# Rotary partners by transfers within SBUF, issued by ACT, and a new order of work around them

## The chip, the cores and the metric

One NeuronCore of a Trainium2 chip runs the whole computation. The metric is the device time of one execution in microseconds; less is better. The engines are PE (TensorE, matrix products), DVE (VectorE), ACT (ScalarE), POOL (GpSimd) and SP (SyncE, which here only issues transfers). The on-chip memory SBUF and the accumulators in PSUM are the two places where data stands between instructions.

## The reference

x is 512 tokens by 1024 columns. It goes through one block of a first kind and then two layers of a second kind, all in float32.

```
# first block
u = rmsnorm(x, ln1_g);  q,k,v,pool_in,z,xbc,dt,gate = split(u @ w_in)
y_a = dilated_attention(q,k,v)   # 3 groups (dilation 1, 4, 16) of 6 heads; the groups' outputs o_g = (p @ v) / l
                                 # are mixed by softmax over the groups of lse_g = max + log(l)
y_b = pool_mixer(pool_in);  y_c = ssd_mixer(z, xbc, dt)
x = x + (gates[0]*y_a + gates[1]*y_b + gates[2]*y_c) @ w_o
x = x + conv_ffn(rmsnorm(x, ln2_g));  x = rmsnorm(x, final_g)
# second block, two layers
u = rms_norm(h, attn_norm[l]);  dq,dk,dv,rq,rk,rv,rg,gq,gk,gv,gates = split(u @ w_in_2[l])
dq, dk = partial_rope(rms_norm(dq)), partial_rope(rms_norm(dk))   # first 16 of each 64
rq, rk = apply_rope(rq), apply_rope(rk)                           # all 128
gq, gk = axial_rope(rms_norm(gq)), axial_rope(rms_norm(gk))       # 32 + 32 of each 64
a, r, c = differential_attention, bidirectional_retention, grouped_query_attention
h = h + sum(gates * (a, r, c) @ w_branch) @ w_out
h = h + square(relu(rms_norm(h, mlp_norm[l]) @ w_mlp_in)) @ w_mlp_out

def apply_rope(x, cos_sin):      # halves x1, x2 of a block
    return concatenate([x1 * cos - x2 * sin, x2 * cos + x1 * sin])
```

## The kernel before

**Products.** Activations lie transposed in SBUF, channels on partitions and the 512 tokens along the free dimension. Each float32 product with weights is made of three products of rounded parts (high x high, high x low, low x high). A chunk of weights is 128 x 1024: SP loads it into one of four slots (`load`), ACT rounds it to its high part (`high`, line 715), DVE or, from the second block on and for every other chunk, POOL subtracts to get the low part (`low`, line 720; `low_pool`, line 751), and PE makes 24 matrix products with it in 3 "thirds" of 8. `high` and `low` called for one chunk treat the chunk three further on. Products with weights accumulate in a ring of four PSUM banks (`G`), all other work of PE in a second ring of four (`M`): a group opens when the group four before it in the ring has been read. Each engine executes its own list in order.

**Filling.** The attention parts are chains over PE, DVE and ACT with gaps for PE. So the projections that come later are cut into thirds, and an order written out by hand (`attn_steps`, `ssd_steps`, `gqa_steps`, `diff_steps`, `ret_steps`) says after which step PE makes how many thirds (`fill(n)`). ACT and DVE do their share of a filling chunk when their own list comes to a step by whose mark PE has finished it (`Follow.to`).

**Block 1.** Units u = 0 to 8 of the dilated attention (three groups of three pairs of heads): scores on PE, bias and maxima on DVE (`front`), exponentials with row sums on ACT, normalising on DVE (`normalise`, lines 1729 and 1733: the reciprocal of the sums, then four scalings for each of two heads), transposes on PE, their copies on ACT, the product with v on PE. `logs(g)` transposes max and log of a group; after the last group DVE and ACT form the softmax over the groups (lines 1769 to 1786) and PE spreads it over the heads (`alpha`, line 1564). The SSD scan follows, later the FFN (`ffn_act`, `ffn_dve`), whose first gating chain runs on ACT and DVE while PE makes the second pair of up products.

**A layer of the second block.** Rotated tiles come in three kinds: g (6 tiles, grouped attention), d (8, differential attention) and r (8, retention). The g tiles stand at the head of the layer, with no filling work: rope_pe, rope_act and rope_dve go tile by tile, then v of the grouped attention is copied (line 2851) and its scores begin. The d and r tiles are filling work: the d tiles fall in the grouped attention, the r tiles in the differential attention. For a tile x, ACT copies and scales it from PSUM to `raw` and squares it for the norm, PE forms the sums of squares (`ss`, line 2701, not for r) and multiplies `raw` with a matrix of zeros, ones and minus ones (`rot`, line 2704), which puts into each half of a block the other half. DVE multiplies `raw` with the cosines, the rotated copy in PSUM with the sines (line 2785), adds them and applies the norm's root (`finish`). ACT may overwrite one of the two `raw` buffers for tile x once `finish(x - 2)` is done, which comes on DVE behind the low part of the next chunk.

**The attention parts of a layer.** Grouped and differential attention have 16 steps each: scores on PE, maxima on DVE, exponentials on ACT (line 2914 for the grouped one), weights on DVE, transposes on PE (line 2868), copies on ACT, and per head or pair a product with v. Retention ends with the mean and the variance of each head, two products with a matrix of ones (`mean`, `var`, line 3168).

Of the kernel before, what the change touches and what calls it, by code (L numbers as in the profile page):

```python
# [25 lines left out]
P = 128  # L26
S = 512
# [36 lines left out]
def const_pack():  # L64
# [14 lines left out]
    def rot(n, half, block):  # L79

        r = np.zeros((P, P))
        for b in range(0, P, block):
            for j in range(half):
                r[b + j, b + j + half] = -1.0
                r[b + j + half, b + j] = 1.0
        return r.T
    put("rot_d", rot(16, 8, 64))
    put("rot_r", rot(128, 64, 128))
    put("rot_g", rot(32, 16, 32))
# [31 lines left out]
def rope_pack():  # L121
# [6 lines left out]
    out[0, :, 0] = 1.0  # L128
    a = table(t, 16, 500000.0)
    for b in (0, 64):  # L130
        out[0, b:b + 16, 0] = np.cos(np.concatenate([a, a]))
        out[0, b:b + 16, 1] = np.sin(np.concatenate([a, a]))
    a = table(t, 128, 10000.0)
    out[1, :, 0], out[1, :, 1] = np.cos(np.concatenate([a, a])), np.sin(np.concatenate([a, a]))
    for b in (0, 64):
        for o, q in ((0, t // 64), (32, t % 64)):
            a = table(q, 32, 10000.0)
            out[2, b + o:b + o + 32, 0] = np.cos(np.concatenate([a, a]))
            out[2, b + o:b + o + 32, 1] = np.sin(np.concatenate([a, a]))
# [94 lines left out]
def attn_steps(score, turned, value, logs, vturn, dtturn, alpha, fill):  # L234

    for u in range(10):
# [21 lines left out]
    logs(2)  # L258
    fill(6)
# [5 lines left out]
def ssd_steps(bturn, xturn, decay, seg, pair, yturn, fill):  # L265

    bturn(0)
    fill(1)
    bturn(1)
    fill(2)  # L270
# [3 lines left out]
    for n in range(18):  # L274
# [9 lines left out]
        fill(1 if n < 11 else 0)  # L284
# [18 lines left out]
def order_block1():  # L303
# [29 lines left out]

    def pair(c, x):
# [6 lines left out]
    attn_steps(score, turned, lambda v: M.add("o", v), lambda g: M.add("lT", g), lambda: [M.add("vt", t) for t in range(NT)],  # L341
# [63 lines left out]

def diff_steps(score, turned, value, mean, fill):

    for u in range(20):
# [7 lines left out]
        fill(2 if u < 17 else 0)  # L416
# [4 lines left out]
def ret_steps(score, value, mean, var, fill):  # L421
# [14 lines left out]
    fill(2)  # L436
    var(3)
    fill(2)
# [29 lines left out]
def order_layer(c1, g1, m1, first):  # L468
# [7 lines left out]
    def post(kind, t):  # L476
        if kind != "r":
            M.add("ss", kind, t)
        M.add("rot", kind, t)
# [109 lines left out]
def build(nc, a, out, consts, attn_consts, ropes, dists, line_dram):  # L589
# [435 lines left out]
    def merge_act(st, n, kt, l=None, final=False):  # L1025
        e, m0 = st.e, merge_count(n, l)

# [372 lines left out]
    lT = kb("lT", [HG, 3, S], 94)  # L1400
    lx = kb("lx", [HG, 2, S], 100)
# [87 lines left out]
    def attn_pe(pe, fill):  # L1489
# [17 lines left out]
        def turned(v, m):  # L1507
            pe.wait_ge(sem("prob_ready"), 2 * v + m + 1)
# [24 lines left out]
        def logs(g):  # L1533
# [67 lines left out]
    def attn_act(st, follow):  # L1601
# [49 lines left out]
        dt_log_act(st)  # L1651
        follow("al", 0)
        for g in range(3):
            e.wait_ge(sem("lmax_ready"), g + 1)
            st.f(e.activation(lT[:, g, :], lT[:, g, :], ACT.Exp), sem("lexp_ready"), g + 1)
        for m in range(3):
# [17 lines left out]
    def attn_dve(st, follow):  # L1674
# [48 lines left out]
        def normalise(v):  # L1723
            g, t = v // 3, v % 3
            w = 256 if g == 0 else P
            for m in range(2):
                h = 2 * t + m
                e.wait_ge(sem("exp_ready"), 2 * v + m + 1)
                st.s(e.reciprocal(stat[:, g, 2, :, h], stat[:, g, 1, :, h]))
# [4 lines left out]
                st.w()  # L1734
                e.sem_inc(sem("prob_ready"), 1)

        def logs(g):
# [3 lines left out]
            gr.done(st, e.tensor_copy(perm(lT[:, g, :], DIL[g]), res(o[0:HG, :], DIL[g])))  # L1741

        for u in range(10):
            if u > 0:
                normalise(u - 1)
                if u % 3 == 0:
                    g = u // 3 - 1
                    e.wait_ge(sem("ln_ready"), g + 1)
# [1893 lines left out]
```

## Time and profile before

| | |
|---|---|
| median of 3 runs | 3173.43 us (3172.94 to 3173.64) |
| the profiled execution | 3172.14 us, of which the span of the trace is 3170.2 us |
| PE busy | 96% of the span, 13152 matrix instructions |
| DVE, ACT, POOL busy | 49%, 40%, 12% |
| mean granted clock of TensorE | 0.981 of full speed |

Busy is the time in which an engine executes at least one instruction. Products overlap on PE, so their mean durations add up to more than they cost; the distance from one start to the next is the cost. A wait is idle time of an engine just before an instruction, put down to what ended it.

### The profile page before, as it was taken

What the parts mean: (1) busy time and instruction counts of PE and PEld (TensorE: products, weight loads), DVE (VectorE), ACT (ScalarE), POOL (GpSimd) and SP (SyncE); (2) the same over time, 40 slices, a digit from 0 to 9 for tenths busy, and PEclk for the clock granted to TensorE, in tenths of its full rate; (3) what the DMA queues carried; (4) which work ended last, traced back from release to release, by engine and by line L of the source; (5) the groups of instructions that cost most, each with busy time, mean ns of one, the idle gap of its engine ahead of it and who ended that gap; (6) DMA issues with size and microseconds to landing.
All of it is one profiled execution on the core that took longest, in us unless ns stands there. A gap on an engine that the chain in (4) does not pass through costs nothing. (4 is left out here: it accounts for less than half of the span.)

```text
span 3170.2 us, 35921 instructions
## 1 busy us (share of the span) xinstructions
PE 3037.3 (96%) x13152; PEld 2332.6 (74%) x13152; DVE 1566.0 (49%) x2166; ACT 1257.5 (40%) x1861; POOL 392.6 (12%) x233
## 2 busy tenths in 40 slices
PE   7997899999999998899999999999899999999998
PEld 6876678888778775566676888887556676788887
DVE  3547667545754666545533551434544633453242
ACT  3445325333433454544444432234554453342221
POOL 4000000000000001011111222221101111222221
PEclk9998899999999999999999999999999999999999
DMA  7222113333323331122222333333112222233332
GB/s 187 80 68 60 42 45 94 99 94 102 91 86 103 88 95 47 40 67 67 71 70 68 99 93 99 94 98 94 39 41 80 65 76 67 80 100 100 93 99 86
DMA packets 460160, 259.02 MB, mean 82 GB/s; under 512 B 20202, under 2 KB 452172, under 8 KB 460016
## 3 DMA queue, kind: packets, MB, share of 16 engines
q1 hardware_dynamic: 454064, 246.03, 26.9%
q0 software_dynamic: 5952, 11.13, 1.4%
q8 instruction: 84, 1.38, 0.2%
q14 instruction: 60, 0.49, 0.1%
HBM read 254.98 MB, written 5.64 MB: 82 GB/s over the span
## 5 line engine op out<-in xcount | busy, mean ns | idle before, releaser
L715 ACT ACTIVATE wH<-wR 128x1024 fp32r<-128x1024 f32 (+1 forms) x476 | 491.3, 1032 | 475.3 <-DMA wR<-in_w_mlp_out_dram 196.9
L720 DVE TENSOR_TENSOR wL<-wR,wH 128x1024 fp32r<-128x1024 f32 (+1 forms) x332 | 396.0, 1193 | 509.0 <-ACT wH L715 492.6
L751 POOL TENSOR_TENSOR wL<-wR,wH 128x1024 fp32r<-128x1024 f32 (+1 forms) x144 | 346.0, 2403 | 2002.9 <-ACT wH L715 2002.9
L782 PE MATMUL ps<-uH,wH 128*128 128x512 f32 x1176 | 483.9, 411 | 5.0 <-DVE wL L720 3.6
L782 PE MATMUL ps<-uL,wH 128*128 128x512 f32 x1176 | 482.7, 410 | 0.0
L782 PE MATMUL ps<-uH,wL 128*128 128x512 f32 x1176 | 479.4, 408 | 0.0
L770 PE MATMUL ps<-uH,wH 128*128 128x512 f32 x976 | 386.0, 395 | 8.8 <-DVE wL L720 7.5
L770 PE MATMUL ps<-uL,wH 128*128 128x512 f32 x976 | 381.2, 391 | 0.0
L770 PE MATMUL ps<-uH,wL 128*128 128x512 f32 x976 | 380.9, 390 | 0.0
L782 PEld LDWEIGHTS ps<-uH,wH 128*128 128x128 f32 x1176 | 226.7, 193 | 78.7 <-issue 24.2
L782 PEld LDWEIGHTS ps<-uH,wL 128*128 128x128 f32 x1176 | 226.9, 193 | 71.3 <-issue 26.1
L782 PEld LDWEIGHTS ps<-uL,wH 128*128 128x128 f32 x1176 | 226.7, 193 | 70.6 <-issue 26.3
L770 PE MATMUL ps<-mH,wH 128*128 128x512 f32 x688 | 268.0, 390 | 2.1 <-DVE wL L720 2.1
L770 PE MATMUL ps<-mL,wH 128*128 128x512 f32 x688 | 267.8, 389 | 0.0
L770 PE MATMUL ps<-mH,wL 128*128 128x512 f32 x688 | 267.8, 389 | 0.0
L770 PEld LDWEIGHTS ps<-uH,wH 128*128 128x128 f32 x976 | 183.9, 188 | 56.6 <-DVE wL L720 16.9
L770 PEld LDWEIGHTS ps<-uL,wH 128*128 128x128 f32 x976 | 183.9, 188 | 38.6 <-issue 1.4
L770 PEld LDWEIGHTS ps<-uH,wL 128*128 128x128 f32 x976 | 183.8, 188 | 38.6
L770 PEld LDWEIGHTS ps<-mH,wH 128*128 128x128 f32 x688 | 129.2, 188 | 29.7 <-DVE wL L720 2.9
L770 PEld LDWEIGHTS ps<-mL,wH 128*128 128x128 f32 x688 | 129.2, 188 | 26.8
L770 PEld LDWEIGHTS ps<-mH,wL 128*128 128x128 f32 x688 | 129.2, 188 | 26.7
L3412 ACT ACTIVATE mH<-msc 128x512 f32 x64 | 40.5, 632 | 235.7 <-DVEq L3448 235.7
(469 smaller groups left out, 4266.4 us busy)
## 6 DMA issues: line engine op xcount, KB each, us to landing
wR<-in_w_in_dram SPq DMA_DIRECT2D x185, 512.0 KB, 3.7
wR<-in_w_mlp_in_dram SPq DMA_DIRECT2D x64, 512.0 KB, 4.0
wR<-in_w_mlp_out_dram SPq DMA_DIRECT2D x64, 512.0 KB, 4.0
wR<-in_ffn_w_up_dram SPq DMA_DIRECT2D x44, 512.0 KB, 3.8
wR<-in_w_branch_dram SPq DMA_DIRECT2D x24, 512.0 KB, 3.4
wR<-in_w_out_dram SPq DMA_DIRECT2D x16, 512.0 KB, 4.1
wR<-in_ffn_w_down_dram SPq DMA_DIRECT2D x16, 384.0 KB, 3.4
wR<-in_ffn_w_down_dram SPq DMA_DIRECT2D x16, 320.0 KB, 3.0
```

The costliest lines, as they stand in the source:

```text
L715: st.f(st.e.activation(wH[:, slot, 0:n], wR[:, slot, 0:n], ACT.Copy), hi_ready, c + 1)
L720: st.f(st.e.tensor_tensor(wL[:, slot, 0:n], wR[:, slot, 0:n], wH[:, slot, 0:n].bitcast(F32), ALU.subtract), lo_ready, c + 1 if done is Non ...
L751: e.tensor_tensor(wL[:, slot, 0:n], wR[:, slot, 0:n], wH[:, slot, 0:n].bitcast(F32), ALU.subtract).then_inc(sem("lo_pool"), 1)
L770: ins = pe.matmul(outp, w[:, k, c0:c0 + m], x[:, k0 + k, :], start=k0 == 0 and s == 0, stop=k0 + kt == kn and s == len(steps) - 1)
L782: ins = pe.matmul(o[:, :], w[:, k, :], x[:, k, :], start=s == 0, stop=s == 3 * KD - 1)
L3412: st.f(e.activation(mHf[:, ds((4 * i + j) * S, S)], msc[:, j % 2, :], ACT.Copy), sem("hidH_ready"), x + 1)
```

## The change

The three rotation matrices leave the constants. The signs go into the sine table, and the exchange of halves is done by transfers from `raw` to a new buffer `partner`, issued by ACT right behind the copy and square of a tile: two per block, so 8 for a g tile, 4 for a d tile, 2 for an r tile. DVE's `finish` waits for them and reads `partner`. For the r tiles the buffer is `sg`, which the gates use otherwise, so two waits are added there.

In the dilated attention the weights are no longer normalised before their product with v. The reciprocal of the row sums is taken once for each group, transposed like the logs (`rT`), and multiplied into the factors of the groups. The logs of the last group move ahead of the last unit.

The rest moves work: thirds in `ssd_steps`, `diff_steps`, `ret_steps`; in `gqa_steps` each step begins with the transposes of two steps before, and its scores come after the first third; in the FFN two weight conversions go from behind the first gating chain to right behind the norm.

```diff
@@ attn_steps
+        if u == 9:
+            logs(2)
+            fill(2)
         turned(u - 1, 0)
-        fill(2 if u < 9 else 3)
+        fill(2)
         turned(u - 1, 1)
...
-    logs(2)
-    fill(6)
+    fill(5)
@@ ssd_steps
     bturn(0)
-    fill(1)
+    fill(2)
     bturn(1)
-    fill(2)
+    fill(3)
...
-        fill(1 if n < 11 else 0)
+        fill(1 if n < 9 else 0)
@@ gqa_steps
     for u in range(19):
-        if u < 16:
-            score(u)
-        fill(1)
         if u >= 6 and u % 4 == 2:
             value(u // 4 - 1)
         if 2 <= u < 18:
             turned(u - 2)
+        fill(1)
+        if u < 16:
+            score(u)
         fill(1)
@@ diff_steps
-        fill(2 if u < 17 else 0)
+        fill((1 if u % 4 == 1 else 2) if u < 17 else 0)
@@ ret_steps
     mean(3)
-    fill(2)
+    fill(5)
     var(3)
-    fill(2)
+    fill(3)
@@ merge_act
+        if l is not None and n == 0:
+            e.wait_ge(sem("rope_done"), 22 + 22 * l)
@@ attn_pe
         def turned(v, m):
-            pe.wait_ge(sem("prob_ready"), 2 * v + m + 1)
+            pe.wait_ge(sem("exp_ready"), 2 * v + m + 1)
...
+            gr = M("rT", g)
+            o = gr.open(pe)
+            for n in range(NT):
+                ins = pe.transpose(o[0:HG, n * P:(n + 1) * P], stat[:, g, 2, n, :], C("ident"))
+            gr.close(ins)
@@ attn_act: the exponentials of lT now stand before dt_log_act and follow("al", 0)
@@ attn_dve
-        def normalise(v):
...
-                for n in range(4):
-                    x = scores_at(v)[:, m, n * w + (P if g == 0 and n == 0 else 0):(n + 1) * w]
-                    st.s(e.tensor_scalar(x, x, stat[:, g, 2, n, h:h + 1], None, ALU.mult))
...
+            if u > 0 and u % 3 == 0:
+                g = u // 3 - 1
+                e.wait_ge(sem("ln_ready"), g + 1)
+                st.s(e.reciprocal(stat[:, g, 2, :, :], stat[:, g, 1, :, :]))
...
+            if u == 9:
+                logs(2)
...
+        st.w()
+        for g in range(3):
+            st.s(e.tensor_tensor(lT[:, g, :], lT[:, g, :], rT[g][:, :], ALU.mult))
@@ ssd_dve: spread(0) moves ahead of the four xt steps
@@ ffn_act
                     normed_u_act(st, u_base("ffn"), 0, G("up", 0, 0, 1))
+                    high(st, ("up", 0, 0, 1))
+                    high(st, ("up", 0, 1, 0))
@@ ffn_dve: low(...) for the same two
@@ rope_post_pe
-        g = M("rot", kind, t, l=l)
         o = g.open(pe)
-        g.close(pe.matmul(o[:, :], C(ROT[kind]), raw[kind][:, x % 2, :], start=True, stop=True))
+        g.close(pe.matmul(o[:, :], C("blk64"), sq[:, x % 2, :], start=True, stop=True))
...
+    HALVES = {"d": (8, (0, 64)), "r": (64, (0,)), "g": (16, (0, 32, 64, 96))}
+    def swap_act(st, kind, x, l):
+
+        half, firsts = HALVES[kind]
+        src, dst = raw[kind][:, x % 2, :], partner[kind][:, x % 2, :]
+        for f in firsts:
+            for a, b in ((f, f + half), (f + half, f)):
+                st.e.dma_start(dst[a:a + half, :], src[b:b + half, :]).then_inc(sem(f"partner_in{x % 2}"), 16)
@@ rope_act, g tiles 0 and 1
                 e.sem_inc(sem("raw_tile"), 1)
+                swap_act(st, kind, x, l)
                 if x > 0:
                     root(x - 1)
@@ rope_act, the other tiles
             e.sem_inc(sem("raw_tile"), 1)
+            if kind == "r" and x == 0:
+                e.wait_ge(sem("sg_free"), 2 + merge_count(2, l) + 8)
+            swap_act(st, kind, x, l)
             if norm and x > 0:
                 root(x - 1)
             high(st, (kind, t), l)
@@ rope_dve
         def finish(x):
...
-            g.done(st, e.tensor_tensor(raw[kind][:, x % 2, :], o[:, :], table[:, S:2 * S], ALU.mult))
-            st.w()
-            st.s(e.tensor_tensor(y, y, raw[kind][:, x % 2, :], ALU.add))
+            e.wait_ge(sem(f"partner_in{x % 2}"), partner_in(kind, x, l))
+            st.w()
+            st.s(e.tensor_tensor(z, z, table[:, S:2 * S], ALU.mult))
+            st.w()
+            st.s(e.tensor_tensor(y, y, z, ALU.add))
@@ gqa_act, gqa_dve: each step in the order of the new gqa_steps (copies of the transposes, then exponentials)
```

## Rows read from the trace of the kernel before

**Rows 1.** The page, busy time of each engine over the whole span.

```profile
PE 3037.3 (96%) x13152; PEld 2332.6 (74%) x13152; DVE 1566.0 (49%) x2166; ACT 1257.5 (40%) x1861; POOL 392.6 (12%) x233
```

**Rows 2.** Busy time in one window: us, then each engine's busy us (instructions), clock.

```profile
1900.00:2000.00 100.00, 100.00 (x443) 82.86 (x442) 22.04 (x26) 20.36 (x20) 21.54 (x9) 1.00 0.33 95
```

**Rows 3.** Waits of PE, whole span: us in total, times, longest.

```profile
PE ps L1564 <- DVEq L1788: 14.9, 1, 14.9
PE ps L3168 <- ACT nrmt L3190: 12.0, 2, 6.2
PE ps L1528 <- ACTq L1648: 11.2, 3, 7.4
PE ps L2868 <- DVE raw L2785: 10.6, 6, 2.9
...
PE ps L2701 <- ACT gpr L2914: 7.6, 6, 2.2
...
PE ps L2868 <- ACT gpr L2914: 6.3, 3, 2.9
PE ps L2027 <- DVEq L2114: 5.5, 3, 2.3
...
PE ps L2704 <- ACTq L2765: 3.3, 2, 1.8
```

**Rows 4.** Line 2704: ns minimum/median/maximum of one, first and last start.

```profile
L2704 PE MATMUL ps<-raw,cn x56: 592/592/1061, 1196.2 to 2349.6; 128*128 128x512 f32 x56
...
L2704 PE MATMUL ps<-raw_r,cn x32: 590/592/697, 1489.1 to 2545.3; 128*128 128x512 f32 x32
```

**Rows 5.** Timeline of PE at 1208 us: start, us, engine, line, count.

```profile
1207.99 1.02 PE L2701 MATMUL ps<-sq,cn 128*128 128x512 f32 x2
1208.85 1.02 PE L2704 MATMUL ps<-raw,cn 128*128 128x512 f32 x2
```

**Rows 6.** Timeline of SP's first issues.

```profile
0.75 0.39 SPq L1178 DMA_DIRECT2D cn<-table_consts_dram  x1
1.19 0.36 SPq L1179 DMA_DIRECT2D grow<-in_ln_g_dram  x1
```

**Rows 7.** Timeline of POOL, two small issues in one row.

```profile
13.72 0.96 POOL L1189 DMA_DIRECT2D prow<-in_gqa_k_norm_dram  x2
```

**Rows 8.** DMA issues: size of one, median us to landing.

```profile
cn<-table_consts_dram SPq DMA_DIRECT2D x1, 64.0 KB, 1.9
```

**Rows 9.** Timeline of ACT in the head of the first layer.

```profile
1193.80 0.63 ACT L2746 ACTIVATE sq<-raw 128x512 f32<-128x512 f32 x1 [1.84 <-DVEq L2800]
...
1198.33 1.06 ACT L715 ACTIVATE wH<-wR 128x1024 fp32r<-128x1024 f32 x1 [0.18 <-ACT rs L878]
1203.13 0.69 ACT L2760 ACTIVATE raw<-ps,lp 128x512 f32<-128x512 f32 x1 [3.73 <-DVEq L2793]
...
1223.72 0.69 ACT L872 ACTIVATE rs<-ps,cn 128x512 f32<-128x512 f32 x1 [2.15 <-PE ps L2701]
...
1227.43 0.60 ACT L2851 ACTIVATE gvf<-ps 128x512 f32<-128x512 f32 x1
```

**Rows 10.** Busy time in two stages of the first layer, columns as in rows 2.

```profile
1229.00:1390.00 161.00, 144.16 (x578) 87.73 (x579) 87.70 (x135) 81.23 (x151) 15.75 (x7) 0.94 0.14 40
1390.00:1580.00 190.00, 186.85 (x773) 130.56 (x770) 99.27 (x148) 84.97 (x144) 30.07 (x14) 1.00 0.25 73
```

**Rows 11.** Groups of DVE by line: busy us, mean ns.

```profile
L1733 DVE TENSOR_SCALAR sc<-sc,stat 128x128 f32<-128x128 f32 (+1 forms) x64 | 15.2, 302 | 0.9
...
L1783 DVE RECIPROCAL lx<-lx 6x512 f32<-6x512 f32 x1 | 3.3, 3342 | 0.0
...
L1786 DVE TENSOR_TENSOR lT<-lT,lx 6x512 f32<-6x512 f32 x3 | 1.9, 674 | 0.0
```

**Rows 12.** Timeline of ACT at the first gating chain of the FFN.

```profile
815.39 1.06 ACT L715 ACTIVATE wH<-wR 128x1024 fp32r<-128x1024 f32 x1
```

**Rows 13.** Timeline of PE at the same place.

```profile
818.24 0.79 PE L770 MATMUL ps<-uH,wH 128*128 128x512 f32 x1 [7.04 <-DVE wL L720]
```

More of the change, by code:

```diff
@@ L332, in turned, with logs @@
             M.add("t", v, m, b)
+    def logs(g):
+        M.add("lT", g), M.add("rT", g)
     def pair(c, x):
@@ L340, in order_block1 @@
     none = lambda n: None
-    attn_steps(score, turned, lambda v: M.add("o", v), lambda g: M.add("lT", g), lambda: [M.add("vt", t) for t in range(NT)],
+    attn_steps(score, turned, lambda v: M.add("o", v), logs, lambda: [M.add("vt", t) for t in range(NT)],
                lambda: M.add("dtT"), lambda m: [M.add("al", m, g) for g in range(3)], none)
@@ L1400, in build @@
     lT = kb("lT", [HG, 3, S], 94)
+    rT = [kb(f"rT{g}", [HG, S], (72, 76, 88)[g]) for g in range(3)]
     lx = kb("lx", [HG, 2, S], 100)
@@ L1655, in attn_act @@
             st.f(e.activation(lT[:, g, :], lT[:, g, :], ACT.Exp), sem("lexp_ready"), g + 1)
+        dt_log_act(st)
+        follow("al", 0)
         for m in range(3):
@@ L1764, in attn_dve @@
                 dt_front_dve(st)
-        dt_mid_dve(st)
-        logs(2)
-        st.w()
-        st.s(e.tensor_tensor(lx[:, 0, :], lT[:, 0, :], lT[:, 1, :], ALU.max))
-        st.w()
-        st.s(e.tensor_tensor(lx[:, 0, :], lx[:, 0, :], lT[:, 2, :], ALU.max))
-        st.w()
-        for g in range(3):
-            st.s(e.tensor_tensor(lT[:, g, :], lT[:, g, :], lx[:, 0, :], ALU.subtract))
-            st.w()
-            e.sem_inc(sem("lmax_ready"), 1)
         follow("al", 0)
@@ L1786, in attn_dve @@
             st.s(e.tensor_tensor(lT[:, g, :], lT[:, g, :], lx[:, 1, :], ALU.mult))
+        st.w()
+        for g in range(3):
+            st.s(e.tensor_tensor(lT[:, g, :], lT[:, g, :], rT[g][:, :], ALU.mult))
         st.w()
@@ L2539, in ffn_dve @@
                     normed_u_dve(st, u_base("ffn"), 0, ffn_gain, 1)
+                    low(st, ("up", 0, 0, 1))
+                    low(st, ("up", 0, 1, 0))
                 for t, cv in ((0, cva), (1, cvv)):
@@ L2781, in finish @@
             y = qk[kind][:, order[x], :]
-            g = M("rot", kind, order[x], l=l)
-            o = g.take(e)
+            z = partner[kind][:, x % 2, :]
+            e.wait_ge(sem(f"partner_in{x % 2}"), partner_in(kind, x, l))
             st.w()
-            g.done(st, e.tensor_tensor(raw[kind][:, x % 2, :], o[:, :], table[:, S:2 * S], ALU.mult))
+            st.s(e.tensor_tensor(z, z, table[:, S:2 * S], ALU.mult))
             st.w()
-            st.s(e.tensor_tensor(y, y, raw[kind][:, x % 2, :], ALU.add))
+            st.s(e.tensor_tensor(y, y, z, ALU.add))
             if norm:
@@ L2905, in gqa_act @@
         for u in range(19):
-            if u < 16:
-                follow("gs", u)
-                e.wait_ge(sem("gmax_ready"), 16 * l + u + 1)
-                if u >= 3:
-                    e.wait_ge(misc_ready, M("gt", u - 3, 1, l=l).nth)
-                st.w()
-                for m in range(2):
-                    g = M("gs", u, m, l=l)
-                    g.done(st, e.activation(gpr[:, u % 3, m, :], g.ps[:, :], ACT.Exp, bias=gst[:, u % 3, m:m + 1],
-                                            accum_out=gst[:, u % 3, 2 + m:3 + m]))
-                st.w()
-                e.sem_inc(sem("gexp_ready"), 1)
             if u >= 6 and u % 4 == 2:
@@ L2937, in gqa_act @@
                 e.sem_inc(sem("gt_turned"), 1)
+            if u < 16:
+                follow("gs", u)
+                e.wait_ge(sem("gmax_ready"), 16 * l + u + 1)
+                if u >= 3:
+                    e.wait_ge(misc_ready, M("gt", u - 3, 1, l=l).nth)
+                st.w()
+                for m in range(2):
+                    g = M("gs", u, m, l=l)
+                    g.done(st, e.activation(gpr[:, u % 3, m, :], g.ps[:, :], ACT.Exp, bias=gst[:, u % 3, m:m + 1],
+                                            accum_out=gst[:, u % 3, 2 + m:3 + m]))
+                st.w()
+                e.sem_inc(sem("gexp_ready"), 1)
     def gqa_dve(st, l, follow):
@@ L2941, in gqa_dve @@
         for u in range(20):
+            if u >= 6 and u % 4 == 2:
+                p = u // 4 - 1
+                follow("gpv", p)
+                g = M("gpv", p, l=l)
+                e.wait_ge(sem("bH_ready"), 27 + 20 * l + p + 1)
+                st.w()
+                g.done(st, e.tensor_tensor(bgL[:, p, :], g.ps[:, :], bgH[:, p, :].bitcast(F32), ALU.subtract))
+                st.w()
+                e.sem_inc(sem("b_ready"), 1)
+            if 2 <= u < 18:
+                follow("gt", u - 2)
             if 1 <= u < 17:
@@ L2951, in gqa_dve @@
                 e.sem_inc(sem("gw_ready"), 1)
-            if u >= 7 and u % 4 == 3:
-                p = u // 4 - 1
-                follow("gpv", p)
-                g = M("gpv", p, l=l)
-                e.wait_ge(sem("bH_ready"), 27 + 20 * l + p + 1)
-                st.w()
-                g.done(st, e.tensor_tensor(bgL[:, p, :], g.ps[:, :], bgH[:, p, :].bitcast(F32), ALU.subtract))
-                st.w()
-                e.sem_inc(sem("b_ready"), 1)
             if u < 16:
```

68 lines of the change are left out of this document (27 added, 41 removed).

## The prediction

> **What bounds the kernel now.** I read the page first [rows 1]: PE is busy 96% of the span, DVE about half and ACT 40%. So nearly every microsecond of PE work taken away where PE is never idle comes off the time, and every microsecond that DVE or ACT takes costs nothing unless PE waits for it. A window in the middle of the MLP gives the price of a product: 443 products in 100 us of unbroken work [rows 2], 0.226 us each; a "third" of a filling piece is 8 of them, 1.81 us. Next the list of waits of PE [rows 3], because most of this change moves work in order to shorten one of them. Last the timeline, for what ACT and DVE do in the short stretch at the head of each layer where no filling work exists. There PE, ACT and DVE run as one chain from tile to tile.
>
> **What goes: the rotation products.** The 88 records of line 2704 [rows 4] are 44 products of two records each (22 tiles in each of two layers, an f32 product having two). Their busy time, 46 us, overlaps; a pair starts 0.86 us after the pair ahead of it [rows 5]. That is 44 x 0.86 = 37.8 us of PE. Twelve of the 44 are g tiles, done in the head of a layer where another chain sets the pace, and I count them at nothing; if PE sets the pace there they are 5.2 us a layer. The 16 others of a layer are d tiles (8, during the grouped attention) and r tiles (8, during the differential attention, where PE is nearly never idle).
>
> **What comes: 192 transfers issued by ACT.** A g tile needs 8 (four blocks, two halves), a d tile 4, an r tile 2: 48 + 32 + 16 = 96 a layer. The trace has no transfer issued by ACT. The nearest rows are small ones from SP, 0.39 and 0.36 us each [rows 6], and from POOL, 0.48 us [rows 7]. ACT executes in order, so an issue there is time in which no activation starts. I take 0.41 us, between SP and POOL; the bounds are 0.36 and 0.50. Nothing in the trace excludes a far lower price on ACT, which is a rival below. Data that small lands in about 2 us (64 KB took 1.9 [rows 8]); DVE needs a tile's partner only after ACT has done the next tile's copy, so the landing is hidden, even at twice that.
> The page "DMA: Bandwidth & Descriptors" of the Trainium skill (section "Anatomy of one DMA") puts the dispatch by the sequencer at about 50 ns. SP's rows here are seven times that; by the page's figure the sum below would come to some 3105 us.
>
> **The head of a layer (g tiles).** Before [rows 9]: ACT squares and scales tile 0 from 1193.80 us, the same for tile 1, then takes the root of tile 0 and converts the weights of the fifth product at 1198.33; DVE's low part follows (1.2 us for a full chunk), so PE starts at about 1200.8. After: 8 issues stand behind tile 0's copy and 8 behind tile 1's, both ahead of that conversion: 16 x 0.41 = 6.6 us, so PE starts at about 1207.4. From there each tile runs: ACT's copy and square (1.3), 8 issues (3.3), the root of the tile before (1.4), the weights' high part (0.6 to 1.1), DVE's low part (0.7 to 1.2) and the rotation's end (2.2), after which ACT may overwrite the buffer with the tile after next. The wait of 3.73 us at 1203.13 for DVE shows this chain. Four more tiles add 4 x 3.3 = 13.1 us, 19.7 with the first 6.6. About 4.3 of it disappears in time that ACT spends waiting for PE's sums (2.15 at 1223.72, with two smaller ones) and in the last step, where the copy of v no longer follows rotations. So the copy of v, at 1227.43 before, comes at about 1243: +15 us in each layer. At 0.36 it is +13, at 0.50 +20. In such gaps PE's clock falls to its half level for some products, which the chain mostly hides.
>
> **Grouped attention (d tiles).** Per layer PE loses 8 x 0.86 = 6.9 us of work. PE's rotation groups also leave the ring of four PSUM slots: the 10.6 us in which transposes waited for a rotation's slot to be read by DVE (line 2785) [rows 3] go with them, 5.3 a layer. Against it ACT gets 32 x 0.41 = 13.1 us more. In this stretch ACT is busy 81 of 161 us [rows 10], but its exponentials are what PE waits for (7.6 and 6.3 us in [rows 3]): a tile's copy, issues, root and conversion are one piece of 5.4 us between two exponentials. The new step order brings each transpose forward: three fills after its scores in place of five. Chain: maxima 1.5, exponentials 1.9, weights 1.5 us, against 3 x 1.81 of fill; it holds only when no such piece falls in between. I take 0 for the stage: -12.2 (work and slots) against about +12 (issues that show). Bounds: -12 if all the issues hide, +12 if the shorter lag shows as well.
>
> **Differential attention and retention.** 8 rotations, 6.9 us, where PE was 98% busy [rows 10], and its wait for ACT's raw r tile (3.3 in two layers, line 2704 [rows 3]): -8.5 a layer. The two issues of an r tile, 0.8 us, lie under the filling work. Four thirds move from the differential steps to the end of retention: mean(3) is followed by 5, not 2, and var(3), for which PE waited 12.0 us in two layers [rows 3], gets 3 x 1.81 = 5.4 us more cover: -5.4 and about -0.6 for the half clock after such a gap, -6 a layer. The differential steps keep 7 thirds of 8 in one step of four, and PE waits nearly nothing there, so I count that at 0; without that cover it would be 1.8 a step.
>
> **Block 1.** Attention: normalising goes from DVE: its scalings alone take 15.2 us over nine units [rows 11], with reciprocals and gaps 2.2 us a unit; it stood ahead of the maxima that ACT's exponentials wait for. Two of the three waits of line 1528 (11.2 in all [rows 3]) and one at line 1514 follow such a unit: 3 x 2 = -6. The transposed reciprocals add 12 transposes, at most 3 us, I take +1. The wait for alpha, 14.9 us, looks as if it went altogether, since the logs move up; but DVE's last convolution piece before it ends with a product that PE finishes one third (1.8 us) before alpha. After that DVE needs 4.4 (convolution, silu, low part) and then two additions 1.4, the reciprocal 3.3, three products 1.9 [rows 11] and three more new ones 1.9: with ACT's 0.8 and the gaps between them 14 us, less 1.8: 12.3 left. -2.6. Together -8 (between -14, if alpha's wait goes, and 0). SSD: one third more ahead of each of the first waits, one less in steps 9 and 10, where DVE was already late (5.5 us in three waits of line 2027 [rows 3]): -1 (-4 to +4). FFN: the weights of the fifth up product were converted only at 815.39, behind the whole first gating chain, and PE stood 7.0 us [rows 12, 13]; moved behind the norm they are ready at 811. -7, and -2 for products at half clock after it (the first record lasts 0.79 us in place of 0.39): -9. Block 1: -18.
>
> **Sum.** A layer: +15 + 0 - 8.5 - 6 = +0.5. Both layers and block 1: +1 - 18 = -17. From the profiled execution, 3172.1 us (span 3170.2), this is 3155; the median of the runs shown is 1.3 above it, so **3156 us**, 0.5% faster.
>
> **Rivals.** (1) Issues on ACT cost next to nothing. Then the head of a layer stays as it is (0), the grouped attention gives -10, the rest -14.5: 2 x -24.5 - 18 = -67, 3106 us. For it: no row of the trace rules it out. Against it: SP and POOL both show 0.36 us or more for the smallest. 13%. By the 50 ns of the Trainium skill this would be the likeliest case. (2) Slower: ACT becomes the bound of the grouped attention. The place is the piece of copy, issues, root and conversion in front of an exponential; price: 1.6 us of issues and 1.4 of the lost lag for each of 8 tiles, 12 us a layer over my sum; with issues at 0.50 in the head, 5 more. 3156 + 2 x 17 = 3190 us. It decides from about 12 us a layer above my forecast. For it: PE's waits for line 2914; against it: ACT is half idle there. 20%. (3) The gains of block 1 are paid back in the layers, the stage sums a few us worse than mine: 3173 us, 16%. It needs the head at +20 and grouped attention at +4. (4) The forecast, 3130 to 3166 around 3156: 51%.
>
> **How the numbers follow.** No change that this kernel's measurement can tell is within 0.2%, 3167 to 3180 us. Faster: (4) and (1), 64%. Same: (3), 16%. Slower: (2), 20%. The range leaves out the cheap end of (1) and the dear end of (2): 3106 to 3188.
>
> **What would show it.** ACT's queue should show transfers 0.4 us apart; in the head, the copy of v should come some 15 us later behind the first g tile than before (34 us then). From the first score of grouped attention to the first of differential attention it should take about what it took, 165 us (1228.7 to 1393.5 us). The retention's wait for line 3168 should fall from 6 to about 0.5 us, the FFN's 7.0 to 0, alpha's from 14.9 to about 12. Transfers landing in 5 us or more, or issues far from 0.41 us, would make the forecast wrong.

## The result, and the profile after

The changed kernel takes 3239.7 us (median of 4 runs, 3235.8 to 3241.9) against 3173.5 us on the same chip: a ratio of 1.0207, 95% interval 1.0189 to 1.0225. It is 66 us slower. The forecast was 3156 us, range 3106 to 3188: wrong in sign and outside its range.

The page of the profiled execution (3241.9 us, granted clock 0.966), against [rows 1]:

```profile
span 3240.1 us, 35849 instructions
...
PE 3039.5 (94%) x13076; PEld 2339.8 (72%) x13076; DVE 1538.9 (47%) x2085; ACT 1260.6 (39%) x1863; POOL 391.3 (12%) x233
```

PE is busy as long as before, with 76 matrix instructions fewer: what it lost in work it got back in products at half clock (326 of its products with weights last over 0.6 us, where 220 did before), and 68 us of idle time came on top (the span's 69.9 less 2.2). ACT's busy time is unchanged too, because issuing a transfer isn't counted as busy in these profiles. So the busy times hide the cause; the timeline of ACT at the head of the first layer shows it (columns as in [rows 9], which are the same instructions before):

```profile
1187.47 0.63 ACT L2759 ACTIVATE sq<-raw 128x512 f32<-128x512 f32 x1 [1.84 <-DVEq L2817]
1188.13 0.72 ACT L2761 ACTIVATE raw<-raw,lp 128x512 f32<-128x512 f32 x1
1188.96 5.10 ACTq L2717 DMA_DIRECT2D partner<-raw  x8
1194.11 0.63 ACT L2759 ACTIVATE sq<-raw 128x512 f32<-128x512 f32 x1 [5.25 <-issue]
...
1195.60 5.00 ACTq L2717 DMA_DIRECT2D partner<-raw  x8
1200.64 0.69 ACT L867 ACTIVATE rs<-ps,cn 128x512 f32<-128x512 f32 x1 [5.15 <-issue]
...
1206.96 0.69 ACT L2774 ACTIVATE raw<-ps,lp 128x512 f32<-128x512 f32 x1 [3.74 <-DVEq L2810]
1207.55 0.59 ACT L2775 ACTIVATE sq<-ps 128x512 f32<-128x512 f32 x1
1208.23 5.00 ACTq L2717 DMA_DIRECT2D partner<-raw  x8
...
1247.49 0.60 ACT L2868 ACTIVATE gvf<-ps 128x512 f32<-128x512 f32 x1
```

Eight issues take 5.0 to 5.1 us, 0.63 us each, and the next activation starts only behind them ("5.25 <-issue"). The copy of v comes 60.0 us after the first squaring; it was 33.6.

The waits of PE over the whole span, against [rows 3] (us in total, times, longest):

```profile
PE ps L3002 <- ACT dpr L3037: 26.0, 4, 7.8
PE ps L2885 <- DVEq L2979: 21.4, 6, 5.2
PE ps L765 <- POOL wL L746: 15.6, 2, 7.8
PE ps L1567 <- DVEq L1782: 14.5, 1, 14.5
PE ps L777 <- DVE wL L715: 13.9, 2, 6.9
PE ps L2899 <- ACT gpr L2951: 11.5, 8, 2.0
PE ps L2703 <- ACTq L2763: 11.0, 2, 5.5
...
PE ps L777 <- POOL wL L746: 10.5, 2, 5.4
PE ps L1526 <- ACTq L1651: 8.9, 3, 5.6
...
PE ps L765 <- DVE wL L715: 5.5, 4, 2.0
...
PE ps L765 <- DVE cva L2553: 3.3, 1, 3.3
```

Gone are the waits that the change aimed at: var(3) (line 3168 before, 12.0), the rotation's slot (10.6), the 7.0 of the FFN. New are four waits of the differential attention's scores for the exponentials (line 3002, 26.0), six of the transposes for DVE's weights (line 2885, 21.4), and those of the heads (lines 765, 777 and 2703, each twice). The wait for alpha (line 1567) is as long as it was.

Grouped and differential attention of the first layer, against [rows 10]:

```profile
1251.00:1425.00 174.00, 148.85 (x569) 92.55 (x568) 81.13 (x136) 80.21 (x149) 14.14 (x6) 0.89 0.14 40
1425.00:1619.00 194.00, 180.94 (x730) 126.85 (x729) 92.02 (x145) 85.31 (x145) 30.36 (x14) 0.96 0.28 79
```

In the second row (differential attention) PE has 13 us idle where it had 3, and a mean clock of 0.96 in place of 1.00. In the first (grouped attention) it has 25 us idle where it had 17, and 0.89 in place of 0.94.

The table cuts each profiled execution at the same instructions: block 1 ends with ACT's squaring of the first g tile, the head with the copy of v, grouped attention with the first score of the differential one, that with the first score of retention, and retention (with the merges behind it) with the first product with w_out. Layer columns are means of the two layers. One execution of block 1 differs from another by some 1.5 us. The 95% intervals of the ratios below are 4 to 6 us to either side, so differences of a few us between two runs rest on the stages of single profiled executions and are no more than indications.

| | block 1 | head | grouped | differential | retention |
|---|---|---|---|---|---|
| before | 1193.8 | 33.6 | 164.5 | 191.4 | 188.9 |
| after | 1187.5 | 60.2 | 174.5 | 194.3 | 187.8 |
| forecast for after | 1175.8 | 48.6 | 164.5 | 365.8 with retention | |
| order_only | 1189.4 | 33.8 | 156.5 | 195.5 | 187.8 |
| transfers_only | 1192.4 | 59.2 | 184.7 | 190.7 | 188.5 |
| g_on_pe | 1187.6 | 33.9 | 172.4 | 193.7 | 187.9 |
| d_on_pe | 1186.8 | 33.8 | 154.9 | 194.0 | 187.8 |
| sp_issue | 1188.4 | 39.6 | 153.0 | 190.7 | 187.9 |
| one_issue | 1189.8 | 35.8 | 158.1 | 191.0 | 187.8 |
| g_twice | 1187.7 | 90.7 | 173.9 | 193.4 | 187.8 |
| g_pe_sp | 1187.7 | 33.8 | 154.7 | 191.5 | 187.8 |
| g_pe_sp_dr0 | 1187.0 | 33.7 | 153.4 | 190.9 | 188.4 |
| r_sp | 1186.9 | 33.7 | 157.5 | 191.3 | 188.7 |
| d_sp | 1186.1 | 33.6 | 151.8 | 192.1 | 188.4 |
| att_back | 1189.5 | 34.4 | 153.9 | 190.8 | 188.5 |
| alpha_first | 1180.8 | 33.7 | 152.9 | 190.8 | 188.5 |
| alpha_d_sp | 1180.6 | 33.6 | 152.5 | 191.3 | 188.6 |
| bdl_late | 1180.4 | 33.6 | 154.8 | 191.1 | 188.7 |
| r_dve_short | 1179.5 | 33.7 | 153.7 | 183.3 | 188.8 |
| r_late | 1179.1 | 33.7 | 152.4 | 187.2 | 188.3 |

After against before: block 1 -6.3, and for each layer +26.6, +10.0, +2.9 and -1.1, so 2 x 38.4 - 6.3 = +70.5 us; the spans differ by 69.9.

### The profile page after: what moved, and what is told of

The parts are those of the page before. It is cut to its first block and busy times, and to the rows that moved or that the text cites. A ratio compares the mean times of both kernels' runs of the same rounds, so it can differ in the third digit from the quotient of the medians.

```text
span 3240.1 us, 35849 instructions
## 1 busy us (share of the span) xinstructions
PE 3039.5 (94%) x13076; PEld 2339.8 (72%) x13076; DVE 1538.9 (47%) x2085; ACT 1260.6 (39%) x1863; POOL 391.3 (12%) x233
## 3 DMA queue, kind: packets, MB, share of 16 engines
q1 hardware_dynamic: 454064, 245.83, 26.6%
```

## The experiments

### The two halves of the change, each alone

order_only undoes the transfers and keeps every new order; transfers_only is the reverse.

```
 order_only (from the changed kernel)      transfers_only (from the kernel before)
-    swap_act(st, kind, x, l)              +    swap_act(st, kind, x, l)
+    M.add("rot", kind, t)                 -    M.add("rot", kind, t)
+    matmul(o, C(ROT[kind]), raw[...])     -    matmul(o, C(ROT[kind]), raw[...])
```

> The reorderings of the change alone; the rotation products stay on PE, no partner transfer. Theory A (the loss comes from ACT's transfer issues, 0.63 us each): the head of a layer is as before (sq to copy of v 33.6 us), block 1 keeps its measured -6.3, and the stages behind lose what the reordering gives: 3157 to 3170 us. Rival B (the new step orders themselves cost: grouped attention +8 a layer, differential steps +5 for the two new waits for ACT's exponentials, line 3002): 3180 to 3195 us.

> The kernel before with the partner transfers alone, every step order as before. Theory A: the head +26 in each layer, grouped attention some +5 because ACT has 20 us more there, r tiles -8 a layer: about 3173 + 2 x (26 + 5 - 8) = 3219 us. Rival B (the orders carry half of the loss): the head +26 in each layer and the rest a gain, -12 a layer: about 3201 us.

order_only: 3157.9 us, ratio 0.9953 (0.9936 to 0.9970). transfers_only: 3263.8 us, 1.0294 (1.0276 to 1.0311). The new orders gain 14 us; the transfers cost 92 us under the old orders and 82 under the new ones (3239.7 less 3157.9). Theory A holds for order_only, at the lower edge of its range. Both numbers for transfers_only were too low: theory A priced the issues in grouped attention at 5 us, rival B counted a gain there, and the stage grew by 20 (184.7 against 164.5). PE's waits there in transfers_only:

```profile
PE ps L2893 <- ACT gpr L2925: 37.3, 7, 5.9
...
PE ps L2879 <- ACT gpr L2925: 12.8, 2, 6.6
...
PE ps L2697 <- ACT gpr L2925: 10.0, 4, 3.6
```

60 us for one thing, ACT's exponential. In the kernel before it is 20.4: the 7.6 and 6.3 of [rows 3], and one row that the forecast did not count, the same scores as in the first row above:

```profile
PE ps L2882 <- ACT gpr L2914: 6.5, 4, 1.7
```

That is rival (2) of the forecast, at more than its price.

### Which tiles cost it, and is it ACT's time

g_on_pe gives g tiles back to PE, d_on_pe g and d tiles. sp_issue keeps all transfers and lets SP issue them.

```
+ONPE = ("g",)          # d_on_pe: ("g", "d"); a plain exchange as the matrix, the signs stay in the table
 def rope_post_pe(pe, kind, x, l):
...
+    if kind in ONPE:
+        g.close(pe.matmul(o[:, :], C("rot_" + kind), raw[kind][:, x % 2, :], start=True, stop=True))
```

```
 def load(e, name, parts, l=None):         # sp_issue; e is SP
...
     e.dma_start(dst, src).then_inc(raw_ready[slot], 16)
+    # the chunk four back was rotated tile x: its partner is fetched here
+    e.wait_ge(sem("raw_tile"), rope_base(kind, l)[0] + x + 1)
+    swap(e, kind, x, l)
```

> The changed kernel, but the g tiles (the head of a layer) get their partners by a product on PE again; d and r tiles keep their transfers. Theory A: the head falls back from 60.0 to about 33.6 us in both layers: 3240 - 53 = 3187 us. Rival C (the head was lengthened by the new order or by PE's clock, not by the issues): the head stays above 50 us, and the time above 3220.

> The changed kernel with g and d tiles rotated by PE; only r tiles, in the differential attention, get their partners by transfers that ACT issues (two a tile). Theory A: grouped attention falls from 173.6 and 164.8 us to the 156 and 150 of the reordering alone, and the r products saved give up to 3 us a layer: 3183 - 33 = 3150 us, 3145 to 3156. Rival (the loss in grouped attention is the lost slot order or the clock, not d's issues): the stage stays above 165 us and the time above 3170.

> The changed kernel, but all partner transfers are issued by SP, behind the load of the weights four chunks on, in place of ACT. Same transfers, same bytes. Theory A (what costs is ACT's time in issuing): the head falls to 34 to 40 us, and grouped and differential attention lose their new waits for ACT: 3165 to 3185 us. Rival D (what costs is the landing of the transfers, or DVE's wait for it): the head stays near 60 us and the time above 3225.

g_on_pe: 3183.0 us, 1.0034 (1.0021 to 1.0046); the head is back at 33.9 us. d_on_pe: 3151.4 us, 0.9935 (0.9918 to 0.9951); grouped attention falls by another 17.5 us a layer. sp_issue: 3148.2 us, 0.9921 (0.9905 to 0.9938), 92 us less than the changed kernel with the same transfers, and 17 us below theory A's range. That the transfers land late (rival D) is out. SP's timeline shows the same price on its queue:

```profile
1195.19 0.58 SPq L706 DMA_DIRECT2D wR<-in_w_in_dram  x1
1195.82 5.01 SPq L2737 DMA_DIRECT2D partner<-raw  x8
1200.87 0.59 SPq L706 DMA_DIRECT2D wR<-in_w_in_dram  x1
```

5.01 us for eight. SP has the time, since its loads run chunks ahead. The head is still 6 us above the old one. A part of it is DVE's wait for the partners, 6.5 us in the two heads together; the rest stays open:

```profile
DVE partner L2822 <- DMA partner<-raw: 6.5, 4, 3.0
```

The Trainium skill ("DMA: Bandwidth & Descriptors", "Issuing engines are not separate DMA queues") says that transfers of all issuing engines run on the same DMA engines, and that issuing from another engine saves only the sequencer's time, "which is usually small relative to the DMA itself". No run here shows which DMA engines took the transfers. That the sequencer's time is what the move saves agrees with the 92 us. That it is small does not hold here: the eight issues of one g tile take 5.0 us, while one transfer of a whole tile lands 2.9 us after its issue (one_issue, below).

### Is the price one per issue

one_issue makes one transfer of each tile and so leaves the exchange of halves out. g_twice makes two transfers for each one of a g tile.

```
 def swap_act(st, kind, x, l):
-    for f in firsts:
-        for a, b in ((f, f + half), (f + half, f)):
-            st.e.dma_start(dst[a:a + half, :], src[b:b + half, :])
+    st.e.dma_start(dst, src)                                        # one_issue
...
+            for c in ((0, S // 2), (S // 2, S)) if kind == "g" ...  # g_twice: half the columns each
```

> The changed kernel, but each tile's partner is one transfer of the whole tile by ACT (44 issues in place of 192). It leaves the exchange of the halves out: DVE gets the unrotated rows. The bytes of g tiles stay as they are, those of d tiles rise to four times. Theory A (the price is one per issue, on ACT): the head falls from 60.0 to 35 to 38 us, grouped attention from 174 and 168 to 156 and 148: about 3240 - 48 - 38 = 3154 us. Rival E (the price follows the bytes or partitions that an issue describes): the 8 issues of a g tile become one of about 5 us, the head stays near 60 us, and the time above 3220.

> The changed kernel, with each transfer of a g tile split into two of half the columns: 16 issues a tile in place of 8, the same bytes. Theory A (0.63 us an issue on ACT): 96 more issues, 60 us, nearly all on the head's chain: the head goes from 60 to about 88 us in each layer, 3240 + 56 = 3296 us. Rival E (the price follows the bytes): the head stays at 60 to 64 us, 3240 to 3248 us.

one_issue: 3149.6 us, 0.9925 (0.9908 to 0.9941), head 35.8 us. g_twice: 3300.8 us, 1.0408 (1.0391 to 1.0425), head 90.7 us. ACT's rows, the first of each kernel:

```profile
1191.30 0.53 ACTq L2715 DMA_DIRECT2D partner<-raw  x1
```

```profile
1189.18 10.22 ACTq L2718 DMA_DIRECT2D partner<-raw  x16
```

A transfer of 256 KB, alone, costs 0.47 to 0.53 us to issue, one of 16 KB in a row of sixteen 0.64. g_twice puts 48 issues more into a head, and the head grows by 30.5 us: 0.64 each, all of it on the path. Theory A holds within 5 us both times: the price is one per issue, and at these sizes the bytes don't matter.

### The rest of the layers

g_pe_sp has g tiles on PE and the other transfers on SP; g_pe_sp_dr0 has besides the old fill of the two last stages:

```
 def diff_steps(score, turned, value, mean, fill):
-        fill((1 if u % 4 == 1 else 2) if u < 17 else 0)
+        fill(2 if u < 17 else 0)
 def ret_steps(score, value, mean, var, fill):
     mean(3)
-    fill(5), var(3), fill(3)
+    fill(2), var(3), fill(2)
```

> The changed kernel with g tiles rotated by PE (the head as before) and the transfers of d and r tiles issued by SP. The two good halves together: the head 33.7 us in place of the 39.6 of all transfers on SP, the rest as there: 3148 - 12 = 3136 us. Rival: PE's clock or the slots take it back and it stays at 3145 or more.

> The same, with the fill of differential attention and retention put back as it was (two thirds in each half step, two around var(3)). Theory F (the thinner fill makes the two new waits of PE a layer, 5 and 8 us in the changed kernel, with the half clock behind them, and costs more than retention gains): differential attention falls by 7 us more than the 7 us of work returned to it would let it, retention gets its 6 us wait back: 3136 - 9 = 3127 us. Rival G (the new waits come from the slots or from ACT's and DVE's order, whatever the fill): the new waits stay and retention's comes back: 3140 us or more.

3142.4 us, 0.9904 (0.9887 to 0.9920), and 3140.9 us, 0.9897 (0.9880 to 0.9913). g_pe_sp lies 6 us above its number. The old fill makes no difference that can be told: the waits for the exponentials halve (22.1 to 10.4 us), and var(3) has its 11.6 back. That is rival G's number with half of theory F's mechanism: the four thirds were moved from one place where they cover a wait to another, and theory F's 9 us did not come.

From g_pe_sp_dr0, d_sp gives r tiles back to PE, r_sp d tiles, and att_back undoes the attention part of block 1.

> The same base of 3140.9 us, but r tiles are rotated by PE again (d tiles by transfers from SP). Forecast's price of the r products, 8.5 us a layer: 3158 us. Theory J (in differential attention the work that goes turns into PE's waits for the exponentials, so it is worth 1 to 2 us a layer): 3143 to 3145 us.

> The same base, but d tiles are rotated by PE again (r tiles by transfers from SP). Forecast's price of the d products with their slots, 12.2 us a layer: 3165 us. Theory J (grouped attention is held by DVE's and ACT's chain of a step, so they are worth little): 3141 to 3147 us.

> The same base, but block 1's attention is as in the kernel before: probabilities normalised on DVE, logs behind the value products. Forecast's price, 8 us: 3149 us. Theory K (from the stage times, 1 to 3 us): 3142 to 3144 us.

d_sp 3139.6 us, 0.9898 (0.9881 to 0.9914); r_sp 3148.3, 0.9923 (0.9907 to 0.9940); att_back 3145.4, 0.9912 (0.9896 to 0.9929). By the medians the r products are worth nothing, d products 3.7 us a layer, the attention part of block 1 some 4.5 us. The forecast had 8.5, 12.2 (with slots) and 8. Two of these are not firm. A second pair of kernels has the d tiles on PE (d_on_pe) and with SP (g_pe_sp), and there grouped attention takes 154.9 and 154.7 us, so d products are worth 0 to 4 us a layer. Of att_back's 4.5 us its block 1 shows 2.5 (1189.5 against 1187.0), the rest lies in the layers, which it does not touch. d_sp is even 3 us below theory J's number, r_sp lies 1.3 us above J's and att_back 1.4 us above K's.

### The wait for alpha

```
     # DVE, behind the last unit of the attention
-    follow("al", 0)
     e.wait_ge(sem("lexp_ready"), 3)
```

> The best version so far (g tiles on PE, d and r transfers issued by SP, fill of the last two stages as before; 3140.9 us) with one line less on DVE: the convolution pieces no longer stand ahead of the combination's additions, reciprocal and products. Theory H (alpha's 14.5 us wait is DVE's backlog): two pieces of 4.3 us go from the chain, alpha comes 8 to 9 us earlier, its wait falls to about 6, and the time to 3132 us. Rival I (PE then waits for the weights' low part or the convolution's slot instead): the wait only changes its name, 3138 us or more.

alpha_first: 3133.5 us, 0.9879 (0.9863 to 0.9896). PE's wait for alpha:

```profile
PE ps L1595 <- DVEq L1809: 5.1, 1, 5.1
```

14.5 us became 5.1 (theory H). In the changed kernel two convolution pieces stood ahead of the additions on DVE, from 305.45 to 314.6 us:

```profile
305.45 2.32 DVE L1972 SCALAR_TENSOR_TENSOR cvt<-ps,PT,cvt 128x511 f32<-128x511 f32 x3
...
308.78 1.23 DVE L715 TENSOR_TENSOR wL<-wR,wH 128x1024 fp32r<-128x1024 f32 x1 [0.15 <-DVE xc L1939]
310.14 2.32 DVE L1972 SCALAR_TENSOR_TENSOR cvt<-ps,PT,cvt 128x511 f32<-128x511 f32 x3
...
314.61 0.67 DVE L1770 TENSOR_TENSOR lx<-lT 6x512 f32<-6x512 f32 x1
...
316.03 3.34 DVE L1774 RECIPROCAL lx<-lx 6x512 f32<-6x512 f32 x1
```

### Where the r products' time goes

> The base alpha_first with r tiles rotated by PE and d tiles by transfers from SP. Since the r transfers were worth nothing (3139.6 without them against 3140.9 us with them), it should measure as alpha_first: 3132 us, 3129 to 3136. If the r transfers are worth the forecast's 8.5 us a layer, it is 3150.

alpha_d_sp: 3133.3 us, 0.9881 (0.9864 to 0.9897): again nothing for the r products. The next runs ask what takes the time. bdl_late moves DVE's low part of a finished head behind the next step's weights.

> The base is alpha_first (3133.5 us; r tiles by transfers, PE's 10.4 us of waits for the exponentials of differential attention in it). Here DVE makes the low part of a finished head one step later, behind the next step's weights, so that its wait for ACT no longer stands ahead of them. Nothing else is changed. Theory J (PE waits because a DVE and ACT chain of a step takes longer than PE's step): the four waits of 2 to 5 us go or halve, differential attention falls from 190.4 and 191.2 to 186 to 188 us, and the time to 3125 to 3129 us. Rival L (the stage's time is set elsewhere, by the contention of transfers or by PE's clock): the stage stays above 190 us, the time at 3131 to 3136.

bdl_late: 3133.2 us, 0.9877 (0.9860 to 0.9893), and the waits stay at 10.4 us in four. Theory J in this form falls: this piece does not hold PE. The timeline of alpha_first around its longest wait shows another. PE:

```profile
1510.95 2.07 PE L3047 MATMUL ps<-qk_d 64*128 64x512 f32 x2 [4.82 <-ACT dpr L3082]
```

DVE ahead of it; the scores whose maxima it takes at 1508.55 were started by PE at 1505.01:

```profile
1504.85 0.69 DVE L2871 TENSOR_TENSOR qk_r<-raw_r,cs_r 128x512 f32<-128x512 f32 x1 [0.15 <-DVE dpr L3137]
1505.58 1.22 DVE L743 TENSOR_TENSOR wL<-wR,wH 128x1024 fp32r<-128x1024 f32 x1
1506.90 0.69 DVE L2847 TENSOR_TENSOR sg<-sg,cs_r 128x512 f32<-128x512 f32 x1
1507.63 0.69 DVE L2849 TENSOR_TENSOR qk_r<-qk_r,sg 128x512 f32<-128x512 f32 x1
1508.55 1.49 DVE L3148 TENSOR_REDUCE stt<-ps 128x1 f32<-128x512 f32 x2 [0.22 <-DVE qk_r L2849]
```

An r tile's pieces stand ahead of the maxima, ACT's exponential comes behind them, and PE's next scores need the slot that it frees. Two runs test it:

```
 def finish(x):                                   # r_dve_short, for r tiles
-    st.s(e.tensor_tensor(z, z, table[:, S:2 * S], ALU.mult))
-    st.s(e.tensor_tensor(y, y, z, ALU.add))
 def rope_dve(st, kind, l):                       # r_late
-            if x > 0: finish(x - 1)
+            if x > 0: LATE.append(lambda x=x: finish(x - 1))
 def diff_dve(st, l, follow):                     # r_late
     e.sem_inc(sem("dmax_ready"), 1)
+    late()
```

> The base is alpha_first (3133.5 us). DVE leaves out the product and the addition that finish the rotation of an r tile (1.4 us for each of 8 tiles a layer), so r tiles are left unrotated; the transfers, PE's and ACT's work are as before. Theory M (PE's waits in differential attention come from r pieces that stand ahead of the maxima on DVE): the wait of 4.8 us falls by 1.4 to 3 us, the half clock behind it shortens, and the stage goes from 190.4 and 191.2 to 186 to 188.5 us; 3126 to 3130 us. Rival N (something else holds it, such as the order of PE's own groups): the stage stays within 1 us of 191, the time at 3131 to 3136.

> The base is alpha_first (3133.5 us), complete in its computation. DVE's two operations that finish the rotation of an r tile move behind the maxima of the step in which they stood ahead of them; no other order changes. Theory M (PE's wait for the exponentials comes from those pieces ahead of the maxima): most of what leaving them out gave comes without leaving anything out, differential attention 184 to 187 us in place of 190.4 and 191.2, 3120 to 3127 us. Rival O (DVE's total load in the stage counts, not the order): the stage stays above 189 us and the time at 3130 or more.

r_dve_short: 3119.5 us, 0.9833 (0.9816 to 0.9849); differential attention falls to 183.3 us, more than theory M asked for, and PE's wait there to 2.4 us in all. The kernel leaves the rotation of the r tiles out. Why it is more isn't shown; some of the additions that it leaves out take 2.77 us in alpha_first and not 0.69 (the last section has the case). r_late: 3124.8 us, 0.9849 (0.9833 to 0.9866), the stage at 187.2; it is the best complete version, 1.5% faster than before. Its wait:

```profile
PE ps L3057 <- ACT dpr L3092: 7.6, 2, 3.9
```

Against alpha_first's 3133.5, order alone gives 9 of the 14 us that shortening gives. By the stage alone it is 3.6 of 7.5 us a layer. So theory M holds, and DVE's length of a step counts besides.

## Why the prediction was wrong

**The step that decided it** is "I take 0.41 us, between SP and POOL; the bounds are 0.36 and 0.50". An issue on ACT takes 0.63 us in a row of eight. The chain of the head was right: with 0.63 in its working, 16 x 0.63 + 4 x 8 x 0.63 - 4.3 = 25.9 us, where 26.6 were measured and 15 forecast. The rows taken [rows 6, 7] were a few issues at the start of the kernel; a bound from them is a bound on those. The trace of before already had the price of an issue that stands right behind another, in the second of two loads in a row:

```profile
1168.54 0.58 SPq L2641 DMA_DIRECT2D wR<-in_w_in_dram  x1
```

With 0.58 in the same working the head is 23.5 us longer. Both heads together: 23 us of the miss. The 50 ns of the Trainium skill ("DMA: Bandwidth & Descriptors", section "Anatomy of one DMA — SWDGE (gpsimd) path"), which the forecast set beside it for rival (1), stand there for GpSimd's path; no run shows such a price on ACT or SP.

**Grouped attention, "0 for the stage"**, came out at +10.0. Three terms were mis-sized. The issues, "about +12", show at 17.7 (g_on_pe against g_pe_sp: 172.4 and 154.7), nearly all of the 20.2 us that 32 of them take: ACT half idle on average said nothing about them; that nearly every issue stood in front of an exponential or of weights is the likely reason. And the new order, held to be worth nothing or a loss of up to 12, gains 8.0 (order_only). The d products with their slots, 12.2 in the forecast, are worth 3.7 by r_sp against g_pe_sp_dr0 and 0.2 by d_on_pe against g_pe_sp. 17.7 - 8.0 - 3.7 is 6.0; of the other 4 us, 2.1 come with the transfers of the g tiles (174.5 against 172.4 in g_on_pe), and 1.9 stay open. 20 us of the miss in two layers.

**Differential attention and retention, "-8.5 a layer" and "-6 a layer"**, together gave +1.8. The step that failed reads PE's 98% busy as "nearly every microsecond of PE work taken away where PE is never idle comes off the time". PE was that busy because its work just covered the chain of maxima and exponentials; with less work the wait appeared and half clock behind it. The r products were worth 0 (alpha_d_sp against alpha_first). With the chain shortened the stage falls by 7.5 us (r_dve_short against alpha_first, 183.3 and 190.8), and by 3.6 with the order of the chain alone (r_late). That these are the 6.9 us of the r products coming free is an argument: no run has the short chain with the r products on PE, and there the stage might fall as well. The refilling did remove the wait for var(3), and the place that it was taken from, counted "at 0", lost as much or more: in order_only the stage has 7.2 us less work and takes 4.1 us more. 33 us of the miss.

**Block 1, -18**, gave -6.3. FFN: the 7.0 us wait went as said, and the half clock with it. But the fifth product, whose weights are ready at 807.6 us, now waits 3.3 us, until 811.1, for its accumulator, which the first gating chain has to read first, and two later products wait 2.0 and 1.4 us for low parts. So 3.0 came in place of 9. DVE's conversions and PE's wait:

```profile
805.16 2.48 DVE L715 TENSOR_TENSOR wL<-wR,wH 128x1024 fp32r<-128x1024 f32 x2 [0.24 <-ACT wH L710]
```

```profile
811.11 0.47 PE L765 MATMUL ps<-uH,wH 128*128 128x512 f32 x1 [3.30 <-DVE cva L2553]
```

Alpha: the forecast counted the last convolution piece (4.4 us), but let DVE start it as soon as PE's product was there. The piece before it was still running until 310.1 us, 3.1 us later, and behind that the work took 13.1 us where 14 were forecast; the wait is 14.5, not 12.3. The attention part with alpha was forecast at 8: alpha's first product starts at 323.3 us, before at 324.2, so 0.8 came. The three waits of line 1528 and the one of line 1514, from which -6 was to come, went from 14.8 us in all to 12.5 (lines 1526 and 1512 of the changed kernel). SSD gave 2.5, more than its 1. 12 us of the miss.

Sum: 23 + 20 + 33 + 12 = 88, and -17 + 88 = +71, the measured 70.

**The rivals.** (2) was the right one, in both of its places, with 3190 us too low: it kept the gains of differential attention and of block 1 that did not come, and its dearest issue was 0.50. Its other half, the lost lag of the new order, is refuted: that order gains. The range failed for the same reason.

What stays open: why d products are worth 0 to 4 us with SP issuing, when their 6.9 us of PE work and 5.3 us of slot waits are gone. PE's waits for the weights of grouped attention (20.4 us in six in g_pe_sp_dr0, 6.7 in two in d_on_pe) stand in their place; no run was made on them.

## What to carry to other kernels

An issue of a transfer is an instruction on its engine's queue. Count issues, not bytes, at the price of a row of issues (0.63 us here), read that price where one issue stands right behind another, and place them on an engine that runs ahead. Where PE is nearly always busy beside a chain on other engines, expect a wait in place of the work that you take from PE: look for the chain first, and check what stands in front of the chain's next link on DVE. A busy share of 40% on an engine says nothing about whether its next instruction is late.

## What the runs showed of the hardware

A load issued alone on SP takes 0.37 us, right behind another issue it takes 0.58 to 0.61. Each issue in a row of eight partner transfers takes 0.63 us on average, on SP as on ACT. Two rows of SP in sp_issue:

```profile
1493.53 0.38 SPq L706 DMA_DIRECT2D wR<-in_w_in_dram  x1
...
1515.84 0.61 SPq L706 DMA_DIRECT2D wR<-in_w_in_dram  x1
```

The second follows a pair of issues that ended at 1515.80. Why the price rises in a row was not tried, and it is not the same everywhere: the first six issues of the kernel before stand behind each other too and take 0.35 to 0.59 us, the eighth 1.85. It did not depend on size between 16 and 32 KB (rows of sixteen and of eight), and one transfer of 256 KB, alone, cost 0.47 to 0.53.

An addition of 128 x 512 on DVE takes 0.69 us. With both inputs in SBUF, and started while POOL makes a low part, it ends only some 0.55 us after POOL does. The first group of rows is of sp_issue, the second of the kernel before:

```profile
1202.72 2.39 POOL L762 TENSOR_TENSOR wL<-wR,wH 128x1024 fp32r<-128x1024 f32 x1 [32.14 <-ACT wH L726]
1202.94 2.71 DVE L2824 TENSOR_TENSOR qk_g<-qk_g,partner 128x512 f32<-128x512 f32 x1
```

```profile
1227.41 2.38 POOL L751 TENSOR_TENSOR wL<-wR,wH 128x1024 fp32r<-128x1024 f32 x1 [7.65 <-ACT wH L715]
1227.68 0.69 DVE L2785 TENSOR_TENSOR raw<-ps,cs_g 128x512 f32<-128x512 f32 x1
1228.40 1.94 DVE L2787 TENSOR_TENSOR qk_g<-qk_g,raw 128x512 f32<-128x512 f32 x1
```

POOL ends at 1205.11 and 1229.79, the additions at 1205.65 and 1230.34. The product at 1227.68, which reads PSUM, keeps its 0.69 us although POOL runs all the time. In each of the two traces all 22 DVE instructions of this size and kind with both inputs in SBUF that start under POOL's low part end 0.54 to 0.60 us behind it, those that read PSUM (6 and 3) keep 0.69, and the 504 and 516 that POOL does not overlap take 0.70 us or less. How much of the kernel's time this costs was not tried.
